# A two-layer hybrid decoder step on one core: router reordered, scatter in pairs, gate slabs' slots given back by gate tiles, mLSTM weightings ahead of gate products

## What is computed

```
u = rmsnorm(h)
cols = u @ w_in                      # inputs of four mixers + 4 x 1024 gate columns
br = [gdn(..), hgrn2(..), ssd(..), mlstm(..)]          # four token mixers, 256 wide each
merged = sum_n sigmoid(gates[n]) * (br[n] @ w_branch[n])
h = h + merged @ w_out
u = rmsnorm(h)
layer 0:  h = h + (silu(u @ wg) * (u @ wu)) @ wd
layer 1:  logits = u @ w_router                        # 8 experts
          top_v, top_i = top_k(logits, 2);  top_w = softmax(top_v)
          h = h + sum_e combine[:, e] * swiglu(u, wg[e], wu[e], wd[e])
h = h + sigmoid(rmsnorm(h) @ w_ple_gate[l]) * (p[l] @ w_ple[l])
```

## Time and profile before

| | us |
|---|---|
| median of three runs | 2373.72 |
| lowest, highest | 2367.26, 2374.87 |
| profiled execution | 2368.56 |
| its span, first to last instruction | 2366.7 |

### The profile page before, as it was taken

The page is one execution under the profiler, slowest core; times in us unless marked ns, Lnnn a source line. Parts: engine busy times, 40 slices in busy tenths (PEclk is TensorE's granted clock), DMA queues, the critical chain, the costliest instruction groups (busy, mean ns, idle before and its releaser), DMA issues.

```text
span 2366.7 us, 51280 instructions
## 1 busy us (share of the span) xinstructions
PE 2226.0 (94%) x23758; PEld 1511.8 (64%) x23758; DVE 571.7 (24%) x1226; ACT 414.2 (18%) x869; POOL 24.8 (1%) x48
## 2 busy tenths in 40 slices
PE   7998999889999999998999888999999999999987
PEld 5766667556776766766667556666566666666555
DVE  4443454321000024443454322001000010000103
ACT  3312532011000013212532012111101111110111
POOL 0000000000000000000000000000000000000000
PEclk9999999799999999999999798999999999999989
DMA  6221112143333334221112134898898989889850
GB/s 246 90 72 64 55 69 87 67 155 117 125 123 115 135 110 151 74 83 54 54 69 87 68 148 160 312 362 329 343 347 310 377 317 356 327 330 361 308 227 23
DMA packets 64556, 426.49 MB, mean 180 GB/s; under 512 B 7792, under 2 KB 10096, under 8 KB 20304
## 3 DMA queue, kind: packets, MB, share of 16 engines
q1 hardware_dynamic: 60224, 409.66, 46.1%
q0 software_dynamic: 3424, 12.76, 1.4%
q10 hardware_dynamic: 688, 0.72, 0.1%
HBM read 415.54 MB, written 7.58 MB: 179 GB/s over the span
## 4 chain that ended last, share of the span: by engine, by line
PE 90%; DVE 6%; ACT 2%; DMA 1%; issue 1%; DVEq 0%; ACTq 0%
PE PJ L551 32%; PE Q L1084 17%; PE Q L551 8%; PE Q L1112 5%; PE Q L1113 5%; PE Q L1085 3%; PE PJ L648 3%; PE Q L563 2%; PE Q L1130 2%; PE Q L1061 2%; PE Q L536 1%; DMA ring<-in_slabs_dram 1%; PE Q L810 1%; PE Q L558 1%; PE PJ L1093 1%
## 5 line engine op out<-in xcount | busy, mean ns | idle before, releaser
L551 PE MATMUL PJ<-u,ring 128*128 128x320 f32 x2400 | 695.2, 446 | 42.2 <-DMA ring<-in_slabs_dram 20.3
L551 PEld LDWEIGHTS PJ<-u,ring 128*128 128x128 f32 x2400 | 462.4, 195 | 248.2 <-issue 38.7
L1084 PE MATMUL Q<-ring,mix 128*32 128x256 f32 (+1 forms) x4224 | 292.6, 361 | 0.9 <-ACT mix L1540 0.9
L1085 PE MATMUL Q<-mix 128*32 128x256 f32 (+1 forms) x1344 | 283.1, 363 | 0.0
L1084 PEld LDWEIGHTS Q<-ring,mix 128*32 128x32 f32 x4224 | 168.0, 110 | 80.2 <-DVE mix L2230 12.3
L1085 PE MATMUL Q<-ring,mix 128*32 128x256 f32 (+1 forms) x960 | 199.2, 362 | 0.0
L2230 DVE TENSOR_TENSOR mix<-mix,Q 128x256 f32<-128x256 f32 (+1 forms) x72 | 28.7, 399 | 674.0 <-PE Q L1085 389.0
L1084 PE MATMUL Q<-mix 128*32 128x256 f32 (+1 forms) x2688 | 191.0, 364 | 0.5 <-issue 0.5
L1085 PEld LDWEIGHTS Q<-mix 128*32 128x32 f32 x1344 | 141.4, 109 | 10.5
L551 PE MATMUL Q<-u,ring 128*128 128x320 f32 x544 | 147.4, 432 | 0.0
L1084 PEld LDWEIGHTS Q<-mix 128*32 128x32 f32 x2688 | 104.9, 109 | 65.6 <-DVE mix L2230 8.3
(11 more groups left out here) (390 smaller groups left out, 2235.1 us busy)
## 6 DMA issues: line engine op xcount, KB each, us to landing
ring<-in_slabs_dram SPq DMA_DIRECT2D x123, 1024.0 KB, 4.8
ring<-in_xslabs_dram SPq DMA_DIRECT2D x110, 1024.0 KB, 7.2
mix<-in_xslabs_dram SPq DMA_DIRECT2D x106, 1024.0 KB, 7.6
ring<-in_xslabs_dram SPq DMA_DIRECT2D x38, 768.0 KB, 5.6
mix<-in_xslabs_dram SPq DMA_DIRECT2D x26, 768.0 KB, 6.2
sts<-in_st_ssd_dram POOLq DMA_DIRECT2D x2, 1024.0 KB, 8.2
out_ssd_s_dram<-sts POOLq DMA_DIRECT2D x2, 1024.0 KB, 4.1
cst<-in_cst_dram SPq DMA_DIRECT2D x1, 1678.0 KB, 14.8
```

Of the source, the lines that this page charges most:

```text
L551: last = mmul(out, w[:, k - k0, j * 128:(j + 1) * 128], rhs[:, k, :], start=(start and k == k0), stop=(stop and k == k1 - 1))
L1084: mmul(out[TW * t:TW * t + TW, :], xg[:, k, TW * t:TW * t + TW], wa[:, k, :], start=(k == 0), stop=(k == KT - 1))
L1085: last = mmul(out[3 * TW:, :], xg[:, k, TW * a:TW * a + TW], wb[:, k, :], start=(k == 0), stop=(k == KT - 1))
```

## The change

1. Slots of gate slabs are given back by the gate tile that reads them (`slot_free`), all others as before. Three branch-weight slabs per layer are requested two slabs later (`load_order`).
2. DVE does the mLSTM's QW, mask, KW and WT ahead of its two products, KW before WT; TensorE waits for KW ahead of the chunk sums and for WT behind them.
3. The router: five of layer 1's embedding tiles come first; then the logits as eight products with the router weights (padded to 32 columns) as the stationary side, in four column groups, copied out by ScalarE and summed and turned by three thin products; then the sixth embedding tile, the 24 transposes while DVE chooses, the ranks, the last two embedding tiles (in Q0). ScalarE loads the Exp table ahead of its embedding copies; a memset moves up; the first selection comes before the overflow flag, for which TensorE waits only behind the experts. The router weights come into `wsm` by a POOL load within layer 1.
4. Scatters run in pairs in rounds 2, 4, 6 and 8, behind `hid_turn` and ahead of the second half round; DVE adds both ahead of the round's product.

```diff
+        def slot_free(n):
+            l = 0 if n < BASE[1] else 1
+            g, t = divmod(n - BASE[l] - N_PROJ, 5)
+            if 0 <= g < 4 and t < 4:
+                return gat_pe, 36 * l + 8 * g + 2 * t + 2
+            return slab_done, n + 1
+        def load_order(l):
+            n0 = BASE[l] + N_PROJ
+            order = list(range(BASE[l], n0 + N_GATED + N_OUT))
+            for g in range(1, 4):
+                order.remove(n0 + 5 * g + 4)
+                order.insert(order.index(n0 + 5 * g + 6) + 1, n0 + 5 * g + 4)
+            return order + list(range(n0 + N_GATED + N_OUT, BASE[l] + PER_LAYER[l]))
...
-                    sp.wait_ge(slab_done, n - R + 1)
+                    sp.wait_ge(*slot_free(n - R))
...
-            for n in range(BASE[1] + pre):
+            for n in load_order(0) + load_order(1)[:pre]:
...
                 chunk_sums(ml_pe, VTm, KWm)
+                pe.wait_ge(*ml_dve.at(l, "wt"))
                 chunk_out(0, ml_dve, VTm, WT, QW)
...
-                ple_products(n2 + N_OUT)
+                ple_products(n2 + N_OUT, 0, 5 if l else KT)
...
+                            if e and r and r % 2 == 0:
+                                scatter(main, e - 1, 1, r - 2)
+                                scatter(main, e - 1, 1, r - 1)
                             half_round(main, e, 1, r, 1, bank)
-                            if e and r:
-                                scatter(main, e - 1, 1, r - 1)
...
+                    pe.wait_ge(wr_in, 16)
+                    for half in range(2):
+                        for g in range(4):
+                            k = 4 * half + g
+                            u_ready(3 * l + 1, k)
+                            last = mmul(PJ[32 * g:32 * g + 32, 1, 0:T], wsm[:, k, :], u[:, k, :], start=(half == 0), stop=(half == 1))
+                    last.then_inc(*rt_pe.did(0, "part"))
+                    ple_products(n2 + N_OUT, 5, 6)
+                    pe.wait_ge(*rt_act.at(0, "part"))
                     for t, (t0, t1) in enumerate(TT):
+                        last = mmul(PJ[0:t1 - t0, 0, t * 8:(t + 1) * 8].rearrange("p (g i) -> p g i", i=2), selt[:, t0:t1],
+                                    SEL[:, :, 0:4].rearrange("p i g -> p g i"), start=True, stop=True)
+                    last.then_inc(*rt_pe.did(0, "logit"))
...
+                    pe.wait_ge(*rt_act.at(0, "utok0"))
+                    ple_products(n2 + N_OUT, 6, KT)
                     pe.wait_ge(*rt_act.at(0, "utok2"))
                     pe.wait_ge(utok_pad, 1)
-                    pe.wait_ge(*rt_dve.at(0, "flag"))
+                    pe.wait_ge(ple_ev, 8 * (l + 1))
                     start(main)
                     experts()
+                    pe.wait_ge(*rt_dve.at(0, "flag"))
...
+                if l:
+                    av(warm[:, :], warm[:, :], ACT.Exp)
...
                 WT, QW, KWm = ml_wt, tt(3), tt(4)
-                products(2)
...
+                v.tensor_tensor(bt(KWm), bt(Q1[:, :, 0:T]), bcol(wend[:, :, :]), ALU.mult).then_inc(*ml_dve.did(l, "kw"))
+                dve.wait_ge(*ml_dve.at(l, "kw"))
                 dve.wait_ge(*ml_pe.at(l, "kq"))
                 v.tensor_tensor(WT, WT, Q2[:, :, 0:T], ALU.mult).then_inc(*ml_dve.did(l, "wt"))
                 dve.wait_ge(*ml_dve.at(l, "wt"))
+                products(2)
...
+                if l:
+                    v.memset(utok[64:128, 2, :], 0.0).then_inc(utok_pad, 1)
...
                         for r in range(RND):
+                            if e and r and r % 2 == 0:
+                                add_y(main, e - 1, 1, r - 2)
+                                add_y(main, e - 1, 1, r - 1)
                             product(main, e, 1, r, (RND * e + r) % 2)
-                            if e and r:
-                                add_y(main, e - 1, 1, r - 1)
...
+                    start(main)
+                    choose(sel, 0, main, "sel", False)
                     did("cnt", v.tensor_scalar(rt[:, 2, 36:37], rt[:, 1, 36:37], float(CAP), None, ALU.is_gt))
                     did("flag", v.tensor_copy(flag[:, :], rt[:, 2, 36:37]))
```

More of the change, by code:

```diff
@@ L309, in trunk_kernel @@
         pads = Steps(sem("pads"), "zero")
-        utok_pad = sem("utok_pad")
+        utok_pad, wr_in = sem("utok_pad"), sem("wr_in")
         dn_dve = sem("dn_dve")
-        rt_pe = Steps(sem("rt_pe"), "utok logit rank")
+        rt_pe = Steps(sem("rt_pe"), "part logit utok0 utok1 utok2 rank")
         rt_dve = Steps(sem("rt_dve"), "lg max idx idf d s r w2 oh0 oh1 M ohw comb rk0 rk1 RK cnt flag")
-        rt_act = Steps(sem("rt_act"), "utok0 utok1 utok2 e")
+        rt_act = Steps(sem("rt_act"), "part e utok0 utok1 utok2")
         def xpart(n, _a=[0]):
@@ L381, in trunk_kernel, with ple_bank @@
         N_OUTS = [0]
+        def ple_bank(l, t):
+            return Q0 if l and t >= 6 else Q1
+        UTOK = (Q0, Q2, Q1)
         def adds(m):
@@ L492, in _ @@
                 store(o_gdn_p[l], Sp[:, NPB % 2, :, 0:64])
+                if l == DEPTH - 1:
+                    pool.wait_ge(*gp_pe.at(l, "part"))
+                    pool.dma_start(wsm[:], wr_d).then_inc(wr_in, 16)
                 pool.wait_ge(*gd_dve.at(l, "ss"))
@@ L617, in ple_logit, with ple_products @@
                         .then_inc(slab_done if t % 2 else gat_pe, 1)
[L619 to L623, removed]
+                def ple_products(n, t0, t1):
+                    if t0 == 0:
+                        pe.wait_ge(ple_in, 16 * (l + 1))
+                        take(n)
+                    for t in range(t0, t1):
                         if t >= 2:
@@ L1187, in _ @@
                 else:
-                    for t, (t0, t1) in enumerate(TT):
-                        if t == 1:
-                            pe.wait_ge(ple_ev, 8 * (l + 1))
-                        for k in range(KT):
[L1193 to L1200, removed]
+                    pe.wait_ge(wr_in, 16)
[7 more added lines that the diff above has]
+                    pe.wait_ge(*rt_act.at(0, "part"))
+                    for t, (t0, t1) in enumerate(TT):
+                        last = mmul(PJ[0:t1 - t0, 0, t * 8:(t + 1) * 8].rearrange("p (g i) -> p g i", i=2), selt[:, t0:t1],
+                                    SEL[:, :, 0:4].rearrange("p i g -> p g i"), start=True, stop=True)
+                    last.then_inc(*rt_pe.did(0, "logit"))
+                    for t, (t0, t1) in enumerate(TT):
+                        if t == 2:
+                            pe.wait_ge(ple_ev, 8 * l + 6)
+                        for k in range(KT):
+                            last = nc.tensor.transpose(UTOK[t][0:t1 - t0, k // 4, (k % 4) * 128:(k % 4 + 1) * 128], u[:, k, t0:t1], ID[:, :])
+                        last.then_inc(*rt_pe.did(0, f"utok{t}"))
                     pe.wait_ge(*rt_dve.at(0, "M"))
@@ L1530, in _, with take_ple @@
                 n3 = BASE[l] + N_PROJ + N_GATED + N_OUT + 1
-                for t in range(KT):
+                if l:
+                    av(warm[:, :], warm[:, :], ACT.Exp)
+                def take_ple(t):
                     if t == KT - 1:
@@ L1535, in _ @@
                         act.wait_ge(ple_pe, 7 * l + t + 1)
-                    av(plep[:, t, :], Q1[:, t % 2, 0:T], ACT.Copy).then_inc(ple_ev, 1)
+                    av(plep[:, t, :], ple_bank(l, t)[:, t % 2, 0:T], ACT.Copy).then_inc(ple_ev, 1)
+                for t in range(5 if l else KT):
+                    take_ple(t)
                 def take_xg(x, e, c0, bank):
@@ L1616, in _ @@
                 else:
-                    act.wait_ge(*rt_pe.at(0, "utok"))
-                    for t, (t0, t1) in enumerate(TT):
-                        av(utok[0:t1 - t0, t, :].rearrange("p (a c) -> p a c", a=2), (Q0, Q1, Q2)[t][0:t1 - t0, :, :], ACT.Copy)\
-                            .then_inc(*rt_act.did(0, f"utok{t}"))
+                    act.wait_ge(*rt_pe.at(0, "part"))
+                    av(selt[:, :], PJ[:, 1, 0:T], ACT.Copy).then_inc(*rt_act.did(0, "part"))
+                    take_ple(5)
                     act.wait_ge(*rt_dve.at(0, "d"))
                     av(rt[:, :, 24:25], rt[:, :, 24:25], ACT.Exp).then_inc(*rt_act.did(0, "e"))
+                    for t, (t0, t1) in enumerate(TT):
+                        act.wait_ge(*rt_pe.at(0, f"utok{t}"))
+                        av(utok[0:t1 - t0, t, :].rearrange("p (a c) -> p a c", a=2), UTOK[t][0:t1 - t0, :, :], ACT.Copy)\
+                            .then_inc(*rt_act.did(0, f"utok{t}"))
+                    take_ple(6)
+                    take_ple(7)
                     start(main)
```

18 lines of the change are left out of this document (6 added, 12 removed).

## The result

The changed kernel took 2296.39 us, the median of three runs (2290.56 to 2301.28), against 2373.72 before: a ratio of 0.968 with a 95% interval of 0.9635 to 0.9725. The profiled execution is the median one. Its span is 2294.3 us, 72.4 less than the 2366.7 of before. The forecast was 2300, with a range of 2284 to 2320.

The account below looks back on a forecast made before the run. TensorE, busy 94% of 2366.7 us, was taken to bound the kernel. Terms 27 + 9 + 8 + 8.5 + 2.3 + 14 = 69 us off 2368.6 gave 2300; own range 2290 to 2310, with rivals 2284 to 2320.

Parts of the forecast that it names:

- Slabs, 27 forecast: Last gate logits: slots freed by gate tiles end 20.3 us of waits and 7.2 of slow tiles; 27 us, bounds 20 and 27.5.
- Rival C: Gate slabs: they still come late, behind a branch weight on SyncE; the 27 us fail, 2327 us; chance 0.06.
- D: SyncE's queue: branch weights hold it, costing 6.8 us per wait; 2381 us from eight more waits; chance 0.03.
- mLSTM, 9.0 and 8: mLSTM: weightings first end DVE waits, 9.0 us (bounds 8 and 9); half the clock loss returns, 8 us (0 and 17).
- Rival A: Thin work of mLSTM and gather: the clock stays low whatever gaps are closed; 2313 us; chance 0.17.
- Router, 8.5 and 2.3: Layer 1's router: gather starts 8.5 us earlier (bounds 6 and 9); clock returning in the gather gives 2.3 (0 and 3.4).
- Scatter, 14 forecast: Expert rounds: pairs behind the transposes cost 1.25 us instead of 1.76; 28 pairs save 14 us, bounds 8 and 18.
- Rival B: Expert rounds: a scatter's extra 0.34 us is its own and goes along wherever it stands; 2314 us; chance 0.08.
- the second case: Scatter pairs: if 128 to 96 rows also changes tiling mode, each pair pays once more; about 9 us instead of 14.

Follow-up runs that it names:

- the last: The changed kernel plus a gate tile within the mLSTM's thin work, one ahead of the GDN's, and an earlier Sigmoid table load: 2277.16 us, ratio 0.9598 to before.
- the repeat: The changed kernel measured once more, unchanged, with three timed rounds: 2296.63 us, ratio 0.9686 to before.

## Why the prediction was right, step by step

**Slabs, 27 forecast, 26.3 measured alone.** All waits went and the tiles behind them are back at 4.57 us: near the upper end of its bounds, 27.5. Layer 0's mLSTM stretch gave some of it back in that kernel: by windows it stood at the lower level for 23.9 us, 20.5 before, which is 1.7 us of work. Rival C, slabs still late behind a branch weight, and D, weights holding SyncE's queue, have their mark in the waits: none of TensorE on slabs or weights. The plain load order shows more than I knew: the margins that I worked out for the later weights were real, but the reordering they were to pay for wasn't needed.

**mLSTM, 9.0 and 8, measured 9.1 and 7.2.** The wait is the time from SSD norm to chunk sums (17.08 to 12.53 in each layer), the clock the time from there to the output projection, with this part alone (91.85 to 89.64 and 94.57 to 89.63). The half that I took for the clock was a choice between bounds 0 and 17, not worked out, so that its size came near is luck. That it lies between them has a ground: in layer 1 the lower level lasted 23.9 us with the wait and lasts 10.2 without it. Rival A was half right here: these 10.2 us per layer stay, with no wait between the thin matmuls.

**Router, 8.5 and 2.3, measured 8.45 and 3.2.** The order of events came as worked out; the gather starts 18.6 us after the first embedding product, which is what the steps gave. The clock came back almost wholly, near the upper bound of 3.4. That was luck as much as reason: in two kernels with the same work of TensorE ahead of it (plain load order, no early Exp) the clock fell and cost 4.2.

**Scatter, 14 forecast, 16.1 measured alone, 16.4 in the changed kernel.** The mechanism was right, and the term was mis-sized in two places that work against each other. I put 0.1 to 0.2 us for an uncovered weight load, and there is none: 1.07 per pair, not 1.25. And I counted 0.34 for every one of the 56 scatters; but the last of each expert stood ahead of the gather, which leaves the 32-column tiles anyway, and had paid nothing: the round with it takes 9.10 us before, and 9.10 with that scatter alone behind the transposes. 49 x 0.34 is 16.7, within 0.6 of what was measured. Rival B, a price that goes along with the scatter, fell by the single scatters behind the transposes. The Trainium skill, page "TensorEngine Tiling (Array Packing)", Key Properties, says that a change of tiling mode drains TensorE. The runs are in line with it for the 32-column tiles, 0.34 us per visit; for 128 to 96 rows there is no such price, as the 1.07 show, and the 9 us of the second case are out.

**What the sum left out.** 69 us were forecast, 72.4 came in the spans. The stages of the terms together gave 73.3, 4.5 more than the 68.8 forecast for them; the rest is +3.5 in layer 0 ahead of anything that was changed in substance, and -2.6 elsewhere. So the total is nearer to the forecast than the terms, and that is luck, as is the choice of the profiled execution to start from: the medians lie 77.3 apart. Windows of layer 0, first before, then after: the same code, another clock.

```profile
216.00:236.00 20.00, 18.75 (x136) 12.27 (x136) 9.94 (x10) 6.26 (x9) 0.56 (x1) 1.00 0.07 27
```

```profile
216.00:236.00 20.00, 18.30 (x126) 12.48 (x125) 6.89 (x10) 4.23 (x6) 0.56 (x1) 0.77 0.12 36
```

I had given identical code no term and no bound. In the twelve kernels (the last and the repeat not counted) in which TensorE's instructions up to the SSD norm of layer 0 are the same, they took 381.5 to 388.2 us. This is why the time of a whole run could not have separated the parts (by runs they are 28.1, 15.1, 9.7 and 19.5), and the stages could.

## What to carry to other kernels

Find what gives a buffer back: a slot that is counted free by a later consumer than its last reader makes the loads late, and freeing it at the reader was worth 26 us here, the order of the requests nothing. Put work of another tile shape where the array changes shape already; batching it is only the second best. And cut a run into stages at the same instructions before comparing, since the clock moves microseconds about in code that nobody touched.

## What the runs showed of the hardware

- Lower-clock stretches come without a wait. Within thin matmuls (64 rows, most with 8 columns, 1282.16 to 1290.35) TensorE went to the lower level, for 10.2 us, though it never stood idle within them; its last wait, 0.68 us, lies ahead of product 18. Without a full tile among them 15 of 16 stretches had these 10.2 us and one had none; with it, of four stretches, one had none and three had 3.4.
- What sets the place and length of these stretches stays open. Two profiles of one kernel agree within 0.4 us in every stage, and two different kernels (plain load order, no early Exp) agree with each other in layer 0 (381.50 and 381.55) and in the router (29.27 both). But twelve kernels with the same TensorE work in layer 0 took 381.5 to 388.2 us for it, and executions of the changed kernel lie up to 12 us apart (2290.56 to 2302.51) at granted clocks from 0.982 to 0.978. No run here varies the program or the moment alone.
- A visit of the 96-row scatter between two half rounds of 128x32 tiles costs 0.34 us beyond its work, behind the 128x128 transposes nothing.
- A table load of ScalarE cost its own 1.28 us and no more. Timeline of the changed kernel:

```profile
1397.16 0.53 ACT L1292 ACTIVATE rstd<-Q,cst 128x320 f32<-128x320 f32 x1 [0.90 <-PE Q L559]
1397.70 1.28 ACT L1569 ACT_TABLE_LOAD   x1
...
1399.00 0.20 ACT L1569 ACTIVATE warm<-warm 128x1 f32<-128x1 f32 x1
```

The Trainium skill, page "ScalarE: Activation LUTs", section "What ACT_TABLE_LOAD costs", gives about 1283 ns for the load and about 1380 ns for a drain besides. The trace agrees with the first; the next ACTIVATE starts 0.02 us behind the load and the one before ended at its start, so that no drain shows here.
